# Start and end of the expert loop, ScalarE's turn in it, short convolution and group norm of a four-layer program in fp32

## The reference

```python
# _rwkv7_branch, group norm at its end
mean = jnp.mean(o, axis=-1, keepdims=True)
var = jnp.mean(jnp.square(o - mean), axis=-1, keepdims=True)
o = (o - mean) * lax.rsqrt(var + RWKV_GN_EPS) * ln_g.reshape(H, N) + ln_b.reshape(H, N)
...
# _short_conv_branch
gb, gc, h = jnp.split(p, 3, axis=-1)
return (gb * _causal_depthwise_conv(gc * h, dw)) @ w_o
# _hybrid_mixer
return (g_a * y_a.astype(x.dtype) + g_b * y_b + g_c * y_c) @ w_out
# _moe_swiglu
logits = (xf @ w_router).astype(jnp.float32)
top_logit, top_idx = lax.top_k(logits, TOP_K)
...
rank = jnp.arange(n_assign, dtype=jnp.int32) - starts[s_expert]
...
def expert_block(args):
    xs, e = args
    return (jax.nn.silu(xs @ w_gate[e]) * (xs @ w_up[e])) @ w_down[e]
```

## Time and profile before

| | us |
|---|---|
| median of 3 runs | 2259.76 (2258.34 to 2264.13) |
| the profiled execution | 2263.32 |
| its span, first to last instruction | 2261.5 |
| PE busy | 2220.2 (98%) |
| PEld busy | 1929.4 (85%) |
| DVE busy | 1789.3 (79%) |
| ACT busy | 1052.5 (47%) |
| mean granted clock of TensorE | 0.989 of full speed |

### The profile page before, as it was taken

How to read it: one execution, slowest core, us unless ns; L and a number is a source line. 1 busy time by engine, 2 the same in 40 slices (tenths; PEclk the granted TensorE clock), 3 DMA queues, 4 the chain that set the end, 5 groups by cost and what they waited for, 6 DMA issues and landing times.

```text
span 2261.5 us, 39382 instructions
## 1 busy us (share of the span) xinstructions
PE 2220.2 (98%) x15642; PEld 1929.4 (85%) x15642; DVE 1789.3 (79%) x1999; ACT 1052.5 (47%) x1306; POOL 32.3 (1%) x36
## 2 busy tenths in 40 slices
PE   9999999999999999999999999999999999999999
PEld 8999899979999887878778787877888898888998
DVE  4986787768867788888888888888868877578776
ACT  5535410035456477777777777775464000243000
POOL 0000000000000000000000000010000000000000
PEclk9999999999999999999999999999989999999999
DMA  5333467633334599999999999995512555423554
GB/s 211 123 115 128 151 218 235 226 131 131 123 120 153 206 415 363 364 371 358 393 352 371 372 360 383 351 403 214 207 39 94 186 186 185 141 83 108 190 186 148
DMA packets 73808, 514.11 MB, mean 227 GB/s; under 512 B 8176, under 2 KB 8304, under 8 KB 14304
## 3 DMA queue, kind: packets, MB, share of 16 engines
q1 hardware_dynamic: 69248, 493.44, 58.5%
q0 software_dynamic: 4448, 19.06, 2.1%
HBM read 498.84 MB, written 13.63 MB: 227 GB/s over the span
## 4 chain that ended last, share of the span: by engine, by line
PE 83%; DVE 9%; ACT 3%; issue 3%; DMA 1%; DVEq 0%; ACTq 0%; SPq 0%
PE wide L372 28%; PE wide L1239 22%; PE wide L1238 22%; ACT ring_hi L2017 1%; DVE ring_more_lo L2899 1%; PE wide L1564 1%; DMA ring<-in_weights 1%; PE wide L1054 1%; PE wide L1319 1%; PE wide L1046 1%; DVE ring_lo L3007 1%; PE wide L1550 1%; DVE ring_lo L2366 1%; DVE ring_lo L2899 1%; PE wide L1523 0%
## 5 line engine op out<-in xcount | busy, mean ns | idle before, releaser
L372 PE MATMUL wide<-ring_hi,hT_hi 128*128 128x512 f32 x664 | 263.6, 397 | 4.9 <-DVE ring_lo L3007 2.3
L2899 DVE TENSOR_TENSOR ring_more_lo<-ring_more,ring_hi 128x2048 fp32r<-128x2048 f32 x96 | 219.8, 2289 | 57.9 <-ACT ring_hi L2017 57.1
L1239 PE MATMUL wide<-ring_hi,hT_lo 128*128 128x512 f32 x664 | 262.1, 395 | 0.0
L372 PE MATMUL wide<-xT_hi,ring_hi 128*128 128x256 f32 x864 | 243.4, 282 | 1.7 <-DVE xT_lo L2359 1.6
L1979 ACT ACTIVATE gate_s<-wide 128x512 f32<-128x512 f32 x43 | 25.8, 599 | 470.4 <-PE wide L1239 470.4
L1239 PE MATMUL wide<-xT_hi,ring_lo 128*128 128x256 f32 x864 | 243.1, 281 | 0.0
L1238 PE MATMUL wide<-xT_lo,ring_hi 128*128 128x256 f32 x864 | 242.7, 281 | 0.0
L372 PE MATMUL wide<-mix_xT_hi,mix_hi 128*128 128x256 f32 x816 | 238.4, 292 | 3.9 <-DVE xT_lo L2625 1.5
L2899 DVE TENSOR_TENSOR ring_lo<-ring,ring_hi 128x2048 fp32r<-128x2048 f32 x96 | 219.8, 2289 | 25.3 <-ACT ring_hi L2017 24.1
L1239 PE MATMUL wide<-mix_xT_hi,ring_lo 128*128 128x256 f32 x832 | 234.5, 282 | 0.0
L1238 PE MATMUL wide<-xT_lo,mix_hi 128*128 128x256 f32 x816 | 230.1, 282 | 0.0
(11 more groups left out here) (557 smaller groups left out, 4892.9 us busy)
## 6 DMA issues: line engine op xcount, KB each, us to landing
ring<-in_weights SPq DMA_DIRECT2D x316, 1024.0 KB, 4.8
ring_more<-in_weights SPq DMA_DIRECT2D x120, 1024.0 KB, 6.8
xT<-in_weights SPq DMA_DIRECT2D x24, 1024.0 KB, 7.2
routed_x<-xe_tm POOLq DMA_DIRECT2D x13, 512.0 KB, 7.0
ln_row<-in_ln_rows POOLq DMA_DIRECT2D x4, 1024.0 KB, 5.7
xe_tm<-routed_x SPq DMA_DIRECT2D x8, 512.0 KB, 7.3
routed_x<-y_tm SPq DMA_DIRECT2D x7, 512.0 KB, 8.6
x_tm<-in_x SPq DMA_DIRECT2D x1, 1024.0 KB, 5.3
```

Source lines behind the costliest of these rows:

```text
L372: ins = self.pe.matmul(out, lhsT, rhs, start=start, stop=stop)
L1239: return pe.matmul(out, lhsT[1], rhs[0], start=False, stop=stop)
L2899: tt_(lo, w, panel_hi(k).bitcast(F32), ALU.subtract).then_inc(S["panel_split"], 1)
```

## The change

1. The router's matmuls write 128 columns instead of 8 (the columns behind the 8 hold other constants, and are not read back).
2. `one_hot` is made from the ranks directly, before the table of items, and the ranks of both halves of the tokens in one pass. TensorE gathers the first item between the two memory tiles and waits for the table behind them; ScalarE starts before it as well, with the first item's panels. `in_slot` is made in the last item, and turned there. The filler matmuls are gone.
3. TensorE's last item stands behind the loop, without the turning and rounding of a next item's tokens.
4. ScalarE's loop is turned by a step: the loop's end now holds the panels of the next item's chunk 1 and the first Silu, with `y_out` between them, and the table of Silu is loaded once before the loop. `tokens_hi` and `tokens_lo` stand behind the last panel of down.
5. `widen_short(0)` stands behind `ln_std`. SP issues 20 panels before it waits for the number of items.
6. In the mixer the short convolution's product and first two taps are in half 1 at stage 5, its last tap at stage 6.
7. At the end of the group norm ScalarE loads the table and takes the deviation before panel 25, VectorE takes the inverse before the low half of that panel, and TensorE does `gn_wide` between the parts of `mix`. In layer 1 the reciprocal for the memory's norm stands behind the low half of panel 27, and panel 28 before `memory_scaled`.

The core of the diff, in the order SP, PE, ACT, DVE:

```diff
-            first_item(range(RAW.slots - 1))
+            first_item(range(TOKENS_AT))
             sp.wait_ge(S["items_ready"], 1)
             n_items = sp.value_load(table_i[0:1, 0:1], min_val=N_EXPERTS, max_val=ITEMS)
-            first_item(range(RAW.slots - 1, TOKENS_AT))
             sp.wait_ge(S["x_routed"], 16 * (ITEMS + 2 + TOP_K * TT))
...
+            sp.wait_ge(S["xe_in"], n_items * 16)
...
                 mix(0, w0, 1)
+                gn_wide(1)
                 mix(0, w0, 2)
-                gn_wide(1)
                 w1 = mixer_panel(l, 25, 2)
...
-                pe.wait_ge(S["items_ready"], 1)
-                n_items = pe.value_load(table_i[0:1, 0:1], min_val=N_EXPERTS, max_val=ITEMS)
-                pe.wait_ge(S["one_hot"], 1)
-                pe.wait_ge(S["ln_x_done"], 2 * DEPTH - 1)
-                pe.wait_ge(S["attn_read"], MEM_PANELS)
-                gather().then_inc(S["routed_mm"], 1)
-
-                pe.wait_ge(S["one_hot"], 2)
-                for tt in range(TT):
-                    ins = pe.transpose(bank[1][:, tt * P:(tt + 1) * P], in_slot[:, tt, :], ident)
-                ins.then_inc(S["slot_turned"], 1)
-                keep_busy(bank[0][:, 0:P], 8)
-                with pe.Fori(0, n_items) as item:
+                def turn_slots():
+
+                    pe.wait_ge(S["one_hot"], 2)
+                    for tt in range(TT):
+                        ins = pe.transpose(bank[1][:, tt * P:(tt + 1) * P], in_slot[:, tt, :], ident)
+                    ins.then_inc(S["slot_turned"], 1)
+
+                def item_pe(item, more):
+
                     pe.wait_ge(S["xe_lo"], item + 1)
                     wide(0, 0, item)
                     wide(1, 0, item)
-                    pe.wait_ge(S["spread"], 1)
+                    pe.wait_ge(S["attn_read"], MEM_PANELS)
                     for s in range(1, FF_CHUNKS):
                         wide(0, s, item)
                         turn(s - 1, item)
                         if s == FF_CHUNKS - 1:
-                            turn_next(item)
+                            if more:
+                                turn_next(item)
+                            else:
+                                turn_slots()
...
+                pe.wait_ge(S["one_hot"], 1)
+                pe.wait_ge(S["ln_x_done"], 2 * DEPTH - 1)
+                gather().then_inc(S["routed_mm"], 1)
+                beside_split()
+                pe.wait_ge(S["items_ready"], 1)
+                last_item = pe.value_load(table_i[0:1, ITEMS + 2:ITEMS + 3], min_val=N_EXPERTS - 1, max_val=ITEMS - 1)
+                with pe.Fori(0, last_item) as item:
+                    item_pe(item, True)
+                item_pe(last_item, False)
+                pe.wait_ge(S["spread"], 1)
...
-                    router = mid[:, MIDS["router"]]
+                    router = mid[:, MIDS["router"].start:]
                     for tt in range(TT):
                         for kb in range(KB):
-                            ins = pe.matmul(bank[2][:, tt * N_EXPERTS:(tt + 1) * N_EXPERTS], xT[:, kb, tt * P:(tt + 1) * P],
-                                            router[:, kb * N_EXPERTS:(kb + 1) * N_EXPERTS], start=(kb == 0), stop=(kb == KB - 1))
+                            ins = pe.matmul(bank[2][:, tt * P:(tt + 1) * P], xT[:, kb, tt * P:(tt + 1) * P],
+                                            router[:, kb * N_EXPERTS:][:, 0:P], start=(kb == 0), stop=(kb == KB - 1))
...
-                    pe.wait_ge(S["ln_x_done"], 2 * DEPTH - 1)
-                    for tt in range(TT):
-                        memory_tile(1, tt)
-                    moe_pe()
+                    memory_tile(1, 0)
+                    moe_pe(lambda: memory_tile(1, 1))
...
                 gn_square(1)
-                widen_in(l, 25)
                 act.activation(stat[:, 62:63], cst[:, 0:1], ACT.Sqrt)
                 gn_std(1)
+                widen_in(l, 25)
...
                 mixed_hi(0)
+                widen_in(l, 28)
                 if l:
                     memory_scaled()
-                widen_in(l, 28)
                 mixed_hi(1)
...
                 def item_act(item, more):
 
                     act.activation(stat[:, 63:64], cst[:, 0:1], ACT.Silu)
-                    for s in range(FF_CHUNKS):
-                        if s + 1 < FF_CHUNKS:
+                    for s in range(1, FF_CHUNKS):
+                        if s < FF_CHUNKS - 1:
                             widen(GATE_UP[0], s + 1, item)
-                        if s:
-                            hidden_hi(s - 1, item)
+                        hidden_hi(s - 1, item)
                         if s + 1 < FF_CHUNKS:
                             widen(GATE_UP[1], s + 1, item)
                         else:
                             widen("down", s - 1, item)
                         silu(s, item)
-                        if 0 < s < FF_CHUNKS - 1:
+                        if s < FF_CHUNKS - 1:
                             widen("down", s - 1, item)
-                    tokens_hi(item + 1)
                     widen("down", FF_CHUNKS - 1, item)
-                    hidden_hi(FF_CHUNKS - 1, item)
                     if more:
-                        for half in range(2):
-                            widen(GATE_UP[half], 0, item + 1)
-                        for h in range(2):
-                            y_out(item, h)
-
+                        tokens_hi(item + 1)
+                        hidden_hi(FF_CHUNKS - 1, item)
+                        widen(GATE_UP[0], 0, item + 1)
+                        widen(GATE_UP[1], 0, item + 1)
+                        y_out(item, 0)
+                        widen(GATE_UP[0], 1, item + 1)
+                        y_out(item, 1)
+                        first_step(item + 1)
+                    else:
+                        hidden_hi(FF_CHUNKS - 1, item)
+                        act.wait_ge(S["slot_turned"], 1)
+                        act.activation(spread[:], bank[1][:, 0:T].rearrange("p (t k) -> p t k", t=TT), ACT.Copy).then_inc(S["spread"], 1)
+
+                act.activation(stat[:, 62:63], cst[:, 0:1], ACT.Copy).then_inc(S["y_sb"], 2)
                 tokens_hi(0)
-                act.wait_ge(S["slot_turned"], 1)
-                act.activation(spread[:], bank[1][:, 0:T].rearrange("p (t k) -> p t k", t=TT), ACT.Copy).then_inc(S["spread"], 1)
-                act.activation(stat[:, 62:63], cst[:, 0:1], ACT.Copy).then_inc(S["y_sb"], 2)
+                beside_split()
+                widen(GATE_UP[0], 1, 0)
+                act.wait_ge(S["items_ready"], 1)
+                n_items = act.value_load(table_i[0:1, 0:1], min_val=N_EXPERTS, max_val=ITEMS)
+                last_item = act.value_load(table_i[0:1, ITEMS + 2:ITEMS + 3], min_val=N_EXPERTS - 1, max_val=ITEMS - 1)
+                act.activation(stat[:, 61:62], cst[:, 0:1], ACT.Silu)
+                first_step(0)
                 with act.Fori(0, last_item) as item:
                     item_act(item, True)
                 item_act(last_item, False)
                 act.activation(stat[:, 62:63], cst[:, 0:1], ACT.Sqrt)
                 for h in range(2):
                     y_last(h)
-                widen_short(0)
...
-                        copy_tokens(0, mem_kv[:, 0], j, j)
-                    moe_act()
+                    copy_tokens(0, mem_kv[:, 0], 0, 0)
+                    moe_act(lambda: copy_tokens(0, mem_kv[:, 0], 1, 1))
                 ln_std(2 * l + 1)
+                if l:
+                    widen_short(0)
                 if l == 0:
...
-                def short_conv():
+                def short_first():
                     dve.wait_ge(S["proj_read"], 24 * l + N_SHIFT + 5)
                     tt_(s_pad[:, :, SHORT_TAPS - 1:], s_pad[:, :, SHORT_TAPS - 1:], conv_c[:], ALU.mult).then_inc(S["dve_step"], 1)
                     dve.wait_ge(S["dve_step"], made.next("dve_step"))
-                    depthwise(conv_c, s_pad, f"short_dw{l}", SHORT_TAPS, 0, SHORT_TAPS)
+                    depthwise(conv_c, s_pad, f"short_dw{l}", SHORT_TAPS, 0, SHORT_TAPS - 1)
+
+                def short_rest():
+                    depthwise(conv_c, s_pad, f"short_dw{l}", SHORT_TAPS, SHORT_TAPS - 1, SHORT_TAPS)
...
-                    elif tt == 0 and stage == SHORT_STAGE:
-                        short_conv()
...
                         conf_centre()
+                        short_rest()
+                    elif tt == 1 and stage == 5:
+                        short_first()
...
                 gn_scaled(1)
+                gn_inv(1)
                 lower_in(l, 25)
-                gn_inv(1)
...
+                added(0)
+                gated(1)
+                lower_in(l, 27)
                 if l:
                     dve.wait_ge(S["mem_std"], 1)
                     dve.reciprocal(stat[:, 44:44 + TT], stat[:, 42:42 + TT]).then_inc(S["mem_inv"], 1)
-                added(0)
-                gated(1)
-                lower_in(l, 27)
...
```

(8 more changed lines are left out.)

96 lines of the change are left out of this document (38 added, 58 removed).

## The result

The changed kernel took 2237.44 us (median of 4 runs, 2235.77 to 2238.82), the kernel before beside it 2261.95 (4 runs). The ratio is 0.988, with a 95% interval of 0.9845 to 0.9914; a second group gave 0.9894 (0.9867 to 0.9922). The profiled execution took 2236.68 (span 2234.9), 26.6 less than that of before.

What follows compares the result with a forecast made beforehand. TensorE, busy for 98% of the span, was taken as the bound, so only its waits, vain work and low clock could be won. The terms summed to -14.15 us from 2259.76, forecast as 2246, range 2239 to 2255.

Steps and rivals of the forecast that it cites:

- The short convolution: Mixer: moved to half 1, where VectorE has idle time, both TensorE waits for p_inv go; -2.7 us.
- the group norm: Its end, both layers: ScalarE idles 0.47 us for TensorE's sums and the first mix waits that much longer; +0.9 us.
- the router: With 128 columns TensorE's clock no longer falls behind it, -1.8, wider matmuls cost +0.1; sum -1.7 us.
- what stands behind the last item: With ln_std ahead of widen_short(0), TensorE's wait for x_tm goes; -1.2 us.
- the rival that it does nothing: Router: padding to 128 columns leaves the low clock and its 1.8 us; 2247.4 us in all, chance 0.20.
- The last item: Making in_slot there costs +0.5; the next tokens' rounding leaves VectorE ahead of hT_lo, -1.3; together -0.8 us.
- Boundaries between items: 0.66 us of TensorE's 0.77 wait for ScalarE's panels goes at each of 6 boundaries; -4.0 us.
- layer 1's reciprocal: Placed behind the low halves on VectorE, it ends TensorE's wait for the low half; -0.85 us.
- ±2 and not in the sum: Low clock of TensorE may fall elsewhere than before, at 1.8 us a stretch; left out of the summed terms.
- The weights' stream: Rival: DMA bounds the items, so gains at start and boundaries become waits for panels; 2253.4 us, chance 0.10.
- The turned loop: Rival: ScalarE's new order makes waits of 0.25 us at 6 boundaries, -4.0 becomes +1.5; 2251.1 us, chance 0.14.
- The copy of the last item: Rival: instruction fetch for TensorE's separate last item is exposed, 4 transfers cost 27 us; 2273 us, chance 0.06.

Runs made afterwards that it cites:

- a_router8: The changed kernel with the router's matmuls 8 columns wide again; median 2246.44 us, fastest 2241.24, profiled execution 2262.3.
- b_tokens: The kernel before, with only the rounding of the next item's tokens moved behind the last panel of down; ratio 0.9969, 96.31 us an item.
- b_hoist: The kernel before, with only the table of Silu loaded once before ScalarE's loop; ratio 1.0015, 96.05 us an item.
- a_y_last: The changed kernel with both halves of y_out ahead of chunk 1's first panel in the turned loop; median 2245.03 us, 95.41 us an item.
- a_best2: The changed kernel with the old group norm end, output_rows later in the last item, and VectorE's panel split before the product; median 2235.79 us, ratio 0.9869.
- b_again: The kernel before, unedited, timed and profiled once more; 2260.34 us.

## Why the prediction was wrong in size

*Right.* The short convolution (-2.7 against -2.8), the group norm (+0.9 against +1.1, for the reason given: ScalarE idle for the sums), the router and what stands behind the last item came within 0.4 us. The padding acts through the clock, as forecast; the rival that it does nothing fell in two experiments. Where the prediction weighed the Trainium skill ("TensorE: Matmul & The Clock Gate", section "What's actually happening": the gate goes by how busy the array is), the busy time that the profile records does not tell the two apart: in a_router8 TensorE is recorded busy in 8.00 of 8.00 us at a clock of 0.57. What the gate counts is not shown here; that the width decides at this place is.

*Right in its sum, by luck.* The last item (-0.8 against -0.7) has other terms than forecast. `in_slot` cost what was taken for it: TensorE's wait for `ring_lo` there grew by 0.6. The wait for `hT_lo` lost 1.0 and not 1.3. The sum put at nothing that TensorE does six turning matmuls fewer there (two for `in_slot` in place of eight), -0.7, and that 0.4 of it comes back at once, since VectorE's product `gate_s` is not ready so early.

*The failed step* is "Boundaries between items": -4.0 was forecast, and the boundaries with the tokens' move, which that step put at nothing, measured -7.8. It took the wait in brackets (0.77, of which 0.66) for all that an item could win, and the move of the tokens was priced only in "Last item", where a wait is shown. The runs showed 0.39 in each of 7 items for that move (b_tokens): a stall of 0.3 before the last product, without a bracket. The boundary itself brought 0.82 to 0.85 instead of 0.66; b_hoist gives 0.63 of it to the table load, and the rest, 0.2, was not taken apart. The 0.66 was also read as what is left of one wait. It is the difference of two things: the wait of 0.77, worth 1.0 with its slow start, less the stall of 0.4 at `xT_hi`, which the peeled item of the earlier trace rows has as well (1469.55, recorded with 0.50). "The order", named there as a cause beside the load, brought nothing (a_y_last). Tokens and boundary together are 3.8 of the 5.1 us by which the change's own part was undersized. The rest is mainly 0.55 at layer 1's reciprocal, 0.5 at the start and 0.4 at the tail. The first matmul behind a wait is recorded with 0.50 instead of 0.39 and the next start is 0.33 to 0.34 later instead of 0.23, so a wait that goes brings some 0.1 more than its bracket; that explains a part.

*The second failed step* is "±2 and not in the sum" for the clock. With the change's own 19.25 us the forecast would have been 2240.5, inside the range. The other 3.1 us of the miss are not the change's work as far as the positions show: a second group of runs of the same changed kernel had a median of 2239.87, inside the range, so on which side of 2239 it fell was luck. The profile of before had lost 23.9 us to the clock, that of after 12.0, of which the router explains 1.7; by the matmuls' positions the rest was 7.4 us of time. In the second block alone, which is the same code everywhere, the profiles lost 3.4 to 23.9 us in 7 kernels built on before and 3.4 to 34.1 in 9 built on the change. A base of 3 runs (2259.76) was itself 1.5 to 4.3 us below the medians of the larger groups of before (2261.29 to 2264.01).

*The other rivals.* The weights' stream did not bound the items: they became 1.2 us shorter with the DMA share at 0.96 in the row below. The turned loop made no wait of its own. The stall of about 0.4 at the panel `xT_hi` that it has stands in b_hoist's loop too, which is not turned: it comes up where the wait for `ring_more_lo` is gone, and a_best2 took it away. The copy of the last item cost nothing that is seen: 88 instruction packets instead of 84, and no gap at its start (its first matmul is recorded with 0.44 us, the same one in the loop with 0.45). One item of the changed kernel, to the earlier trace rows:

```profile
1058.57:1154.04 95.47, 95.32 (x428) 77.08 (x427) 83.25 (x58) 71.17 (x61) 0.00 (x0) 1.00 0.96 374
```

*Open.* Whether the change makes low clock in the unchanged parts rarer: the medians of what the second block lost are 11.9 us (7 profiles on before) and 6.8 (9 on the change), and single ones overlap wholly. Nor was it found what starts such a stretch.

## What to carry to other kernels

Before pricing a loop, compare each matmul's step and duration with those of its neighbours: a stall of a few tenths has no bracket, but the matmul behind it is recorded longer (0.50 instead of 0.39), and in a loop it counts once a turn. A wait that goes can uncover the next one: here 0.4 of 1.0 us came back at the next panel. A term that comes out right can hide two that were left out, so look at its parts. An engine at 47% can still be the one that is waited for at one place: look at what stands between the last release and the next panel there, a table load first. When parts of the clock's loss change from run to run by more than the edit is worth, judge an edit by the positions of the same instructions, not by the median.

## What the runs showed of the hardware

- TensorE's clock fell within or right behind 32 router records 8 columns wide in 7 profiles of 7 and behind the same 128 columns wide in 0 of 9. The clock's records show 1.7 to 3.4 us lost there; the wider matmuls cost 0.1 (3.71 and 3.81 us for 32).
- The same code in the second block ran at a mean clock of 0.54 for 48 us in one execution (a_router8), while the whole block lost 3.4 us in others. The Trainium skill ("TensorE: Matmul & The Clock Gate", section "What's actually happening") says that where the clock changes varies between runs of one kernel. The traces agree: the low stretch at 1654 to 1671 us is in the first profile of before and not in b_again. The time of one kernel moved by 21 us (a_router8, 2241.24 to 2262.30) and by 30 (b_hoist, 2253.70 to 2283.50).
- A table load of 1.28 us in ScalarE's loop cost 0.63 us an item, two of them at another place 1.73.
- The first 128x512 matmul behind each of TensorE's waits in the items is recorded with 0.50 us instead of 0.39, and the next one starts 0.33 to 0.34 us after it instead of 0.23.
